# The rows of ada's first four blocks, dealt out anew over TensorE, VectorE and GpSimd

## The reference, cut to what matters

```python
c_act = jax.nn.silu(c)
mod = c_act @ ada_w[l] + ada_b[l]
sh1, sc1, g1, sh2, sc2, g2, sh3, sc3, g3 = jnp.split(mod, N_MOD, axis=-1)
h = modulate(rms_norm(x, norm_ffn1[l]), sh1, sc1)
x = x + 0.5 * g1[:, None, :] * swiglu(h, ffn1_w_gate[l], ffn1_w_up[l], ffn1_w_down[l])
```

## Time and profile before

| | us |
|---|---|
| median of 3 runs | 1151.31 |
| lowest and highest | 1150.41 and 1154.48 |
| profiled execution, its time | 1150.95 |
| its span, first to last instruction | 1148.9 |
| TensorE busy | 1131.1 |
| VectorE, ScalarE, GpSimd busy | 738.0, 493.1, 117.2 |

### The profile page before, as it was taken

The page is one execution under the profiler, slowest core; times in us unless marked ns, Lnnn a source line. Parts: engine busy times, 40 slices in busy tenths (PEclk is TensorE's granted clock), DMA queues, the critical chain, the costliest instruction groups (busy, mean ns, idle before and its releaser), DMA issues.

```text
span 1148.9 us, 17467 instructions
## 1 busy us (share of the span) xinstructions
PE 1131.1 (98%) x6378; PEld 988.0 (86%) x6378; DVE 738.0 (64%) x1167; ACT 493.1 (43%) x758; POOL 117.2 (10%) x115
## 2 busy tenths in 40 slices
PE   8899999999999999999999999999999999999997
PEld 7788888888888998888888888889899999988887
DVE  4766665666544666675555666757789899962332
ACT  5232332232222247655645656633445454542232
POOL 3301000000110001102002230000410110100000
PEclk9999999999999999999999999999999999999999
DMA  9567566557677425438236755242334545343331
GB/s 308 171 207 251 193 200 218 167 166 243 211 246 234 126 74 118 111 98 176 85 94 132 158 118 124 76 125 76 101 102 130 146 118 156 95 119 98 91 115 74
DMA packets 244174, 167.95 MB, mean 146 GB/s; under 512 B 6198, under 2 KB 224516, under 8 KB 244116
## 3 DMA queue, kind: packets, MB, share of 16 engines
q1 hardware_dynamic: 227188, 143.48, 41.8%
q0 software_dynamic: 16208, 21.33, 8.9%
q10 hardware_dynamic: 720, 2.36, 0.6%
HBM read 164.99 MB, written 16.05 MB: 158 GB/s over the span
## 4 chain that ended last, share of the span: by engine, by line
PE 90%; DVE 2%; SPq 2%; DMA 2%; issue 2%; ACT 1%; POOL 0%; DVEq 0%; POOLq 0%; ACTq 0%
PE bank L1909 28%; PE bank L1911 28%; PE bank L1910 28%; PE bank L2277 2%; PE bank L2270 1%; PE bank L2293 1%; SPq L604 1%; PE bank L2265 1%; PE bank L2292 1%; DMA raw<-in_ffn_w_gate_dram 1%; SPq L623 1%; DMA adas<-in_ada_w_dram 1%; SPq L617 1%; DVE hL L1298 0%; DVE tmp L1293 0%
## 5 line engine op out<-in xcount | busy, mean ns | idle before, releaser
L1909 PE MATMUL bank<-hH,wH 128*128 128x512 f32 (+1 forms) x976 | 355.3, 364 | 5.2 <-DVE hL L1298 3.3
L1911 PE MATMUL bank<-hH,wL 128*128 128x512 f32 (+1 forms) x976 | 351.2, 360 | 0.0
L1910 PE MATMUL bank<-hL,wH 128*128 128x512 f32 (+1 forms) x976 | 351.0, 360 | 0.0
L810 ACT ACTIVATE wH<-raw 128x1024 fp32r<-128x1024 f32 x131 | 135.8, 1037 | 350.6 <-PE bank L1911 348.0
L1232 DVE TENSOR_TENSOR wL<-raw,wH 128x1024 fp32r<-128x1024 f32 x131 | 156.6, 1195 | 200.5 <-ACT wH L810 199.7
L1909 PEld LDWEIGHTS bank<-hH,wH 128*128 128x128 f32 x976 | 184.1, 189 | 35.0 <-issue 5.3
L1911 PEld LDWEIGHTS bank<-hH,wL 128*128 128x128 f32 x976 | 184.0, 189 | 27.9
L1910 PEld LDWEIGHTS bank<-hL,wH 128*128 128x128 f32 x976 | 184.2, 189 | 26.4
L1909 PE MATMUL bank<-actH,wH 128*128 128x512 f32 (+1 forms) x316 | 120.7, 382 | 0.0
L1911 PE MATMUL bank<-actH,wL 128*128 128x512 f32 (+1 forms) x316 | 120.4, 381 | 0.0
L1910 PE MATMUL bank<-actL,wH 128*128 128x512 f32 (+1 forms) x316 | 120.4, 381 | 0.0
(11 more groups left out here) (276 smaller groups left out, 1928.3 us busy)
## 6 DMA issues: line engine op xcount, KB each, us to landing
adaw<-in_ada_w_dram SPq DMA_DIRECT2D x28, 1024.0 KB, 6.1
raw<-in_mix_w_in_dram SPq DMA_DIRECT2D x41, 512.0 KB, 3.9
raw<-in_ffn_w_down_dram SPq DMA_DIRECT2D x32, 512.0 KB, 4.0
raw<-in_ffn_w_gate_dram SPq DMA_DIRECT2D x25, 512.0 KB, 4.0
raw<-in_ffn_w_up_dram SPq DMA_DIRECT2D x25, 512.0 KB, 4.0
adas<-in_ada_w_dram SPq DMA_DIRECT2D x16, 512.0 KB, 8.0
raw<-in_ffn_w_down_dram SPq DMA_DIRECT2D x16, 384.0 KB, 4.2
wsum_d<-in_ffn_w_gate_dram POOLq DMA_DIRECT2D x8, 704.0 KB, 8.0
```

Source lines behind the costliest of these rows:

```text
L810: nc.scalar.activation(wH[s][:, :n * P], raw[s][:, :n * P], ACT.Copy).then_inc(hi_done, 1)
L1909: T.matmul(o, a[0], b[0], start=start, stop=False)
L1910: T.matmul(o, a[0], b[1], start=False, stop=False)
L1911: return T.matmul(o, a[1], b[0], start=False, stop=stop)
```

## The change

ROWS_PE becomes (4, 5, 6, 7) for all four blocks, so TensorE takes four rows of each. ROWS_P becomes (2, 2, 1, 1): GpSimd does one row, not two, of blocks 2 and 3. VectorE is left with rows 2 and 3 of blocks 0 and 1 and rows 1 to 3 of blocks 2 and 3, all in the first half of a block; its call for rows 4 and 5 of block 0 falls away. `first_sums(3)` moves ahead of tiles(2, 2).

```diff
--- before.py
+++ after.py
@@ -100,10 +100,10 @@
 
 
 
-    ROWS_P = (2, 2, 2, 2)
+    ROWS_P = (2, 2, 1, 1)
 
     CHAINED = (2, 3)
-    ROWS_PE = ((6, 7), (7,), (7,), (6, 7))
+    ROWS_PE = ((4, 5, 6, 7),) * ADA0
     ROWS_V = [DT - len(rows) for rows in ROWS_PE]
     SUMS = [(() if b in CHAINED else (0,)) + (1,) + ((2,) if rows else ()) for b, rows in enumerate(ROWS_PE)]
     STEPS_P = [sum(2 * r - 1 for r in ROWS_P[:b]) for b in range(ADA0 + 1)]
@@ -1301,7 +1301,6 @@
             def normed():
                 every = slice(0, SEQ)
                 diagonals(0, slice(0, TT))
-                first_rows(0, 4, ROWS_V[0])
                 first_prep(0)
                 first_prep(1)
                 dve.wait_ge(bc_done, 1)
@@ -1976,9 +1975,10 @@
                 first_sums(2)
                 tiles(3, 1)
                 first_parts(3)
-                for u in range(3):
-                    tiles(u, 2)
+                tiles(0, 2)
+                tiles(1, 2)
                 first_sums(3)
+                tiles(2, 2)
                 tiles(3, 2)
                 dummies(4, B_ADA_START[2])
                 for u in range(N_FIRST):
```

## The result

| | before | after |
|---|---|---|
| median of 4 runs, us | 1152.89 | 1169.63 |
| lowest and highest | 1150.41 and 1155.14 | 1158.75 and 1172.62 |
| profiled execution, its time (span) | 1150.95 (1148.9) | 1168.82 (1167.1) |
| mean granted clock of the profiled span | 0.998 | 0.985 |

The ratio is 1.0134, with a 95% interval from 1.0104 to 1.0163: slower, and by much more than the 0.6% forecast; 1169.63 lies outside the range. The before of this table has a fourth run (1155.14) beside the three that the forecast started from. One later run of before (1613.23 us) and one of e12 (1613.02), both at a mean clock of 0.653, are left out everywhere. The page of after says

A forecast was written before the change was run, and what follows sets the result against it. The prediction took TensorE, busy 98% of the span, as the bound. To 1151.3 us it added 4.8 for TensorE's longer line and 1.6 for the clock, other parts nothing more: 1157.7 us, range 1153.5 to 1160.7.

The forecast's parts named there:

- What bounds the kernel: TensorE, busy 98% of the span, bounds the kernel; moving its work moves the end unless an idle gap absorbs it.
- Part 1, the added rows: TensorE's 80 added small passes, 8.6 us in blocks 0 to 3, of which 4.8 us stay.
- the roll: TensorE's rows stepped forward at full clock: columns of blocks 0 to 3 start 1.5, 3.3, 4.4 and 4.8 us later.
- three tiles in 3.18: Step for block 2: three tiles take TensorE 3.18 us from 38.2, before the parts, a tile and the sums.
- Parts 2 and 3, VectorE and GpSimd: VectorE's eight removed instructions (6.3 us) and GpSimd's removed row in the last two blocks, both costed at nothing.
- Part 4, the forward sums: Sums of block 3 ahead of the third tile: worth 1.3 us, already included in the 4.8.
- Part 5, the clock: Slower first sums with a late rise, or one more clock fall on TensorE: 1.6 us further in all.
- my upper bound: Block 0's sums go as slowly as dummies at low clock, adding 1.3 us, and the clock's rise is put off.
- several falls: Rival: every long burst of small passes brings a low-clock stretch, +9.5 to +12.8 us; chance 0.10.
- clock harmless: Rival: TensorE bounds, but no clock fall beyond the earlier one, 1156.1 us (+3.5 to +5.7); chance 0.25.
- Not slower: Rival: added passes hide under running matmuls and shorter GpSimd and VectorE chains set the end, about 1147.6 us; chance 0.12.

The follow-up runs named there:

- e12: The e8 kernel with all small passes, sums included, 32 columns wide: 1149.84 us against 1151.87 for before, ratio 0.9981.
- e1: The kernel before plus 16, 24, 24 and 16 large dummy matmuls behind the small passes of blocks 0 to 3: 1156.31 us against 1151.36.
- e6: The kernel after with the passes of blocks 1 to 3 cut into bursts of eight, one behind each tile: 1167.82 us, ratio 1.0095 to before.
- e8: The kernel before with GpSimd doing one row in block 2 and the sums of block 3 moved forward: 1149.23 us against 1151.77.
- e7: The kernel before with only the sums of block 3 moved ahead of tiles(2, 2): 1151.27 us against 1151.77, ratio 0.9993.
- e2: The kernel after with the passes of TensorE's four rows per block 64 columns wide, sums still one column: 1156.64 us against 1151.36 for before.
- e11: The kernel after with all small passes, sums included, 32 columns wide: 1157.65 us, ratio 1.0057 to before.
- e5: The kernel after run once more without any edit: 1164.45 us, ratio 1.0125 to before.
- e10: The kernel after with block 0 as before (two rows on TensorE, rows 2 to 5 on VectorE): 1166.64 us, ratio 1.0157 to before.
- e9: The kernel before with two rows of each block on TensorE, 64 small passes instead of 48: 1151.45 us against 1151.87, ratio 1.0006.
- e3: The kernel after with 4 dummy matmuls behind every eight added passes, 64 in all: 1167.60 us against 1151.36 for before.

## Why the prediction was right or wrong

- **What bounds the kernel**: right. TensorE's line sets the start of the last tiles, and the end follows it (+18.3 and +18.2 in after; in the profiles of the experiments the two differ by up to 1.0 us).
- **Part 1, the added rows**: right within about 1 us. The first three columns' starts of e1 lie within 0.3 us of the roll. Its +4.95 for the roll's +4.8 is closer than the roll deserves, since e1 lacks the forward sums and gets 0.8 us back at the end. Two runs of e6 (1155.5, 1156.5) are 3.7 and 4.7 us above before. The "three tiles in 3.18" of block 2 are two calls of tiles(); the 3.18 us is right.
- **Parts 2 and 3, VectorE and GpSimd**: right to be costed at nothing behind a late TensorE. Where TensorE isn't late, GpSimd's row is worth more than the 0 given here (e8).
- **Part 4, the forward sums**: priced at 1.3 us within the changed kernel, not measured apart there, since the runs scatter more than that (without them e1's fourth columns and last tiles start 1.0 us behind the roll, which has them); alone in the kernel before, not distinguishable from zero (e7).
- **Part 5, the clock**: the step that failed. "I take one further 1.6 us in all" stood there; the profiled run had 27.2 us more at half clock, which at half a microsecond each is 13.6 us. Two things in the step were wrong. I priced a fall as one stretch of 3.4 us, because the one stretch of before was so long; after, the stretches were 10.2, 6.8, 10.2 and 3.4 us, and 20.5 in e6. At half clock a small pass takes 0.214 us, not the 0.187 of my upper bound, so the bursts grow while the clock is down; that this is what keeps it down was not tried apart, but the step left it out. And I weighed the evidence the wrong way: the one burst of that length in the trace had made a fall, those that hadn't were a quarter as long, and still "several falls" got 0.10. Even that rival's +12.8 was short of the +18 in the profile and the +16.7 of the medians, by the length of the stretches. Three of the eight runs of after (1158.8 to 1159.1) do lie in the range: in the one profiled, 6.8 us more at half clock cost 3.4 us. The term fits a run with few falls and fails for the other five.
- **The rivals**: "clock harmless" is what e1 shows for large work; the wide passes of e2 come near it, with three of four runs at mean clocks of 0.996 to 0.998 (0.998 in the profile of before). The rule of the Trainium skill, page "TensorE: Matmul & The Clock Gate", section "Why this matters for your kernels", by which long idle gaps bring the clock down, was not enough: after had 0.38 us of gaps in this stretch and 30.6 us at half clock. The formula of that page's section "LDWEIGHTS (loading the stationary operand)", which has no term for the clock, does not hold either: the f32 loads took 192 ns in the profile of before, at full clock, and 333 in that of after, in the stretch from 19.95 to 30.1 (count, busy us, mean ns):

```profile
L1939 PEld LDWEIGHTS bank<-ones,adasc 128*128 128x128 f32 x8 | 1.8, 333 | 0.0
```

- "Not slower" needed a pass below 0.07 us; it costs 0.107 at full clock and twice that at half.

Left open: why one run has the falls and another not, and what ends a low stretch. Runs of one program differ in where the clock changes; no experiment set that. That fewer streamed columns favour the falls is shown by e2 and e11 against e5 and e10; that nothing else does is not shown, as the fall of e2 at 27.8 us and those of before in e9 tell.

## What to carry to other kernels

Work of single columns is cheap on TensorE only in small doses: besides its place in the line (0.107 us a pass) it can take the clock away from the large matmuls around it, and that cost nearly three times as much in the profiled run (13.6 us against 4.8) as the longer line. Where such passes are needed in number, make their moving operand wider (32 or 64 columns at 0.11 us each), which here made the low stretches fewer but did not end them, and look at the granted clock of several runs, not of one. And when a view shows one clock fall, price what keeps it low, not only the stretch that is seen.

## What the runs showed of the hardware that was not expected

- The price of a small pass hardly depends on its columns: 0.107 us with one, 0.110 with 64. The clock does: of eight runs with one column, five had a mean clock of 0.983 to 0.985; of four with 64 columns and four with 32, all were at 0.994 or above. The other three runs with one column lie at 0.994 to 0.995 as well, so what is missing is the group with some 30 us at half clock.
- In e6 TensorE stayed at half clock for 20.5 us without a gap in its line, the last 4.5 us of it in large matmuls alone; in e2, 32 passes of 64 columns ran at half clock from end to end.
- GpSimd's product of a row took 3.01 us instead of 1.56 (in the profile after; the row of block 3 beside it):

```profile
32.35 3.01 POOL L667 TENSOR_SCALAR adasp<-adas,csilu 128x512 f32<-128x512 f32 x1 [5.07 <-DMA adas<-in_ada_w_dram]
38.37 1.56 POOL L667 TENSOR_SCALAR adasp<-adas,csilu 128x512 f32<-128x512 f32 x1 [3.01 <-DMA adas<-in_ada_w_dram]
```

While the first ran, VectorE was subtracting two tensors in SBUF (L1353, from 31.66 to 34.0); during the second it was idle. The same row took 2.98 us in e3 and 3.00 in e6, beside the same subtraction, and 1.57 in e5, where that was over by 32.2 us. Nobody waited for it.
